# Second attention: the rotary part of the scores as two fp32r products of stacked parts

## The reference, cut to what matters

```
kv = (ckv_all @ w_kvb).reshape(B, Lk, H_D, NOPE_D + V_D)
k_nope, vals = jnp.split(kv, [NOPE_D], axis=-1)
keys = jnp.concatenate([k_nope, jnp.broadcast_to(kpe_all[:, :, None, :], (B, Lk, H_D, ROPE_D))], axis=-1)
qf = jnp.concatenate([q_nope, q_pe], axis=-1)
o_d = block_attention(qf, keys, vals, (NOPE_D + ROPE_D) ** -0.5).reshape(B, L, HALF_W)
```

## Time and profile before

| | us |
|---|---|
| time, three runs | 1636.16, 1636.16, 1636.3 |
| median | 1636.16 |
| span of the profiled execution | 1631.4 |
| median less span | 4.8 |
| TensorE busy | 1590.6 |
| VectorE busy | 1078.2 |
| ScalarE busy | 733.7 |

### The profile page before, as it was taken

One profiled execution on the slowest core, in us unless ns is written; L12 is line 12 of the kernel. 1 busy time (PEld: TensorE's weight loads), 2 busy tenths in 40 slices (PEclk: granted clock), 3 DMA queues, 4 the chain that ended last, 5 costly groups with the idle time before them and its releaser, 6 DMA issues.

```text
span 1631.4 us, 27746 instructions
## 1 busy us (share of the span) xinstructions
PE 1590.6 (98%) x11361; PEld 1464.3 (90%) x11361; DVE 1078.2 (66%) x1872; ACT 733.7 (45%) x1303; POOL 37.1 (2%) x42
## 2 busy tenths in 40 slices
PE   6999999999999999999999999999999999999997
PEld 3588897799989999999999996778999999999997
DVE  5634662868857747856874557744888487587486
ACT  5435363646624414423545433344665154254254
POOL 0000000001000000000003002000100000000000
PEclk9999999999999999999999999999999999999999
DMA  9565423035455544545234202002532223133222
GB/s 320 191 220 187 156 80 101 16 94 119 124 159 156 152 119 128 151 125 155 72 111 149 78 30 77 27 1 60 122 83 85 72 78 99 57 96 86 78 65 91
DMA packets 239336, 178.21 MB, mean 109 GB/s; under 512 B 9429, under 2 KB 232843, under 8 KB 238572
## 3 DMA queue, kind: packets, MB, share of 16 engines
q1 hardware_dynamic: 236276, 171.19, 34.9%
q0 software_dynamic: 2016, 4.59, 2.0%
q10 hardware_dynamic: 920, 0.69, 0.2%
HBM read 163.37 MB, written 8.49 MB: 105 GB/s over the span
## 4 chain that ended last, share of the span: by engine, by line
PE 89%; DVE 3%; ACT 3%; SPq 2%; DMA 2%; issue 1%; ACTq 0%; DVEq 0%
PE ua L1119 7%; PE ub L1119 6%; PE ua L1121 6%; PE ua L1120 6%; PE ub L1121 6%; PE ub L1120 6%; PE ua L1583 6%; PE ua L1585 5%; PE ua L1584 5%; PE ub L1583 5%; PE ub L1585 5%; PE ub L1584 5%; PE pm L1033 2%; PE ua L1428 2%; PE ub L1428 2%; PE pt L1455 1%
## 5 line engine op out<-in xcount | busy, mean ns | idle before, releaser
L2178 ACT ACTIVATE whi<-weight_sums 128x1024 fp32r<-128x1024 f32 x88 | 93.2, 1059 | 72.1 <-DVE weight_sums L2867 47.2
L1583 PE MATMUL ua<-x_mixed_high,whi 128*128 128x322 f32 x352 | 110.6, 314 | 1.9 <-ACT snap L2252 1.9
L1583 PE MATMUL ub<-x_mixed_high,whi 128*128 128x322 f32 x352 | 111.0, 315 | 0.9 <-ACT snap L2252 0.9
L1585 PE MATMUL ua<-x_mixed_high,wlo 128*128 128x322 f32 x352 | 109.2, 310 | 0.0
L1585 PE MATMUL ub<-x_mixed_high,wlo 128*128 128x322 f32 x352 | 109.2, 310 | 0.0
L1584 PE MATMUL ub<-x_mixed_rest,whi 128*128 128x322 f32 x352 | 109.0, 310 | 0.0
L1584 PE MATMUL ua<-x_mixed_rest,whi 128*128 128x322 f32 x352 | 109.0, 310 | 0.0
L2840 DVE TENSOR_TENSOR wlo<-weight_sums,whi 128x1024 fp32r<-128x1024 f32 x88 | 107.2, 1218 | 1.5 <-ACT whi L2178 1.4
L1119 PE MATMUL ub<-hidden_high,whi 128*128 128x384 f32 (+1 forms) x324 | 101.7, 314 | 4.5 <-DVE x L2935 3.5
L1119 PE MATMUL ua<-hidden_high,whi 128*128 128x384 f32 (+1 forms) x324 | 101.1, 312 | 1.9 <-DVE x L2935 1.9
L1121 PE MATMUL ua<-hidden_high,wlo 128*128 128x384 f32 (+1 forms) x324 | 100.1, 309 | 0.0
(11 more groups left out here) (671 smaller groups left out, 4949.0 us busy)
## 6 DMA issues: line engine op xcount, KB each, us to landing
raw<-in_w_ffn_in SPq DMA_DIRECT2D x88, 512.0 KB, 5.6
mod_late<-in_w_mod SPq DMA_DIRECT2D x24, 1024.0 KB, 5.4
raw<-in_w_ffn_out SPq DMA_DIRECT2D x48, 384.0 KB, 4.4
modw<-in_w_mod SPq DMA_DIRECT2D x17, 1024.0 KB, 5.8
raw<-in_w_in_even SPq DMA_DIRECT2D x10, 1024.0 KB, 7.8
raw<-in_w_in_odd SPq DMA_DIRECT2D x7, 1024.0 KB, 5.6
mod_first<-in_w_mod SPq DMA_DIRECT2D x5, 1024.0 KB, 12.3
ssq<-sq POOLq DMA_DIRECT2D x14, 320.0 KB, 4.7
```

The source lines that it names most:

```text
L1583: pe.matmul(dst, wh[:, c], xh, start=first, stop=False, skip_group_check=True)
L1585: ins = pe.matmul(dst, wl[:, c], xh, start=False, stop=last, skip_group_check=True)
L2178: act.activation(ring(whi, g, w), src, ACT.Copy).then_inc(g_hi, 1)
```

## The change

The zero-padded planes go. In their place stand the rotary keys as high part and rest, each with the key in both halves of the rows, and the queries, for each head, as high part in one half of the rows and rest in the other half. A product over all 128 rows of such queries with the keys' high part adds high by high and rest by high; one with the keys' rest adds high by rest and rest by rest. A run of scores in the second attention so has three products, one in fp32 and two in fp32r, where it had two in fp32.

ScalarE gets five more copies behind its 17 (one of the keys, four of queries). VectorE gets five subtractions: those of the keys and of head 0 ahead of the first Hyena tile, those of heads 1 to 3 ahead of the tiles 1 to 3. TensorE waits for all five ahead of the second attention. VectorE writes the rotary keys once in place of twice, and GpSimd's zero fill goes; its count moves to the fill just before it. The new query buffers take the places of `cq` and `sq`, the rest of the keys overwrites the keys.

```
-        kpz = ta("kpz", [P, 2, NKEY])
+        kr_hi = ta("rotary_keys_high", [P, NKEY], F32R)
+        kr_lo = ta("rotary_keys_rest", [P, NKEY], F32R)
+        kr = sb("rotary_keys", [P, NKEY], at=sb_at["rotary_keys_rest"])
...
+        qr = [sb("rotary_queries_even_heads", [P, 2, T], F32R, at=sb_at["cq"]),
+              sb("rotary_queries_odd_heads", [P, 2, T], F32R, at=sb_at["sq"])]
...
             for c in (0, LS + 1, UW - 2):
-                pool.memset(uh[:, :, c:c + 1], 0.0)
-            pool.memset(kpz[:, :, :], 0.0).then_inc(s_zero, 1)
+                ins = pool.memset(uh[:, :, c:c + 1], 0.0)
+            ins.then_inc(s_zero, 1)
...
-            pe.wait_ge(l_rq, 2)
+            pe.wait_ge(l_rq, 2 + 5)
             pe.wait_ge(y_f, 3)
-            attention(1, lambda h, t: [qn[:, h, t], qp[:, h // 2, t]], lambda h, t: [kn[:, h, t], kpz[:, h % 2, t]],
+            attention(1, lambda h, t: [qn[:, h, t], qr[h % 2][:, h // 2, t], qr[h % 2][:, h // 2, t]],
+                      lambda h, t: [kn[:, h, t], kr_hi[:, t], kr_lo[:, t]],
...
+            act.wait_ge(l_rk, 1)
+            act.activation(kr_hi[:, :], kr[:, :], ACT.Copy).then_inc(l_ev, 1)
+            for h in range(4):
+                rows = slice(64 * (h % 2), 64 * (h % 2) + 64)
+                act.wait_ge(l_rq, h // 2 + 1)
+                act.activation(qr[h % 2][rows, h // 2], qp[rows, h // 2], ACT.Copy).then_inc(l_ev, 1)
             for c in range(4):
                 act.wait_ge(y_f, c + 1)
...
-                    for a in range(2):
-                        rows = slice(64 * a, 64 * a + 64)
-                        ins = dve.tensor_copy(kpz[rows, a, 0:PAST], pm[rows, PAST:2 * PAST])
-                    ins.then_inc(l_c, 1)
+                    dve.tensor_copy(kr[:, 0:PAST], pm[:, PAST:2 * PAST]).then_inc(l_c, 1)
...
-            for a in range(2):
-                rows = slice(64 * a, 64 * a + 64)
-                dve.tensor_tensor(kpz[rows, a, PAST:PAST + LS], rot2[rows, 0, :], rot2[rows, 1, :], ALU.add)
-                ins = dve.tensor_copy(kpz[rows, a, PAST + LS:NKEY], kp[rows, LS:T])
-            ins.then_inc(l_rk, 1)
+            dve.tensor_tensor(kr[:, PAST:PAST + LS], rot2[:, 0, :], rot2[:, 1, :], ALU.add)
+            dve.tensor_copy(kr[:, PAST + LS:NKEY], kp[:, LS:T]).then_inc(l_rk, 1)
...
+            def rotary_query_rest(h):
+                rows, across = (slice(0, 64), slice(64, P))[::(1, -1)[h % 2]]
+                dve.wait_ge(l_ev, 17 + h + 2)
+                dve.tensor_tensor(qr[h % 2][across, h // 2], qp[rows, h // 2], qr[h % 2][rows, h // 2].bitcast(F32),
+                                  ALU.subtract).then_inc(l_rq, 1)
+
+            def rotary_rest(c):
+                if c == 0:
+                    dve.wait_ge(l_ev, 17 + 1)
+                    dve.tensor_tensor(kr_lo[:, :], kr[:, :], kr_hi[:, :].bitcast(F32), ALU.subtract).then_inc(l_rq, 1)
+                    rotary_query_rest(0)
+                elif c < 4:
+                    rotary_query_rest(c)
...
             for c in range(4):
+                rotary_rest(c)
                 dve.wait_ge(y_mm, c + 1)
```

More of the change, by code:

```diff
@@ L533, in build_program @@
         l_mm = sem("mla_projected")
-        l_ev = sem("mla_copied")
-        l_rq = sem("mla_queries_rotated")
+        l_ev = sem("mla_copied_and_rounded")
+        l_rq = sem("mla_queries_rotated_and_rests")
         q_ld = m_early[0:4]
```

## The result

The changed kernel takes 1626.6 us (median of four runs, 1625.22 to 1628.91) against 1636.16 us before: the ratio is 0.9947, with a 95% interval of 0.9935 to 0.9959. A second measurement of both gives 1626.31 against 1634.14 us, a ratio of 0.9949 (0.9934 to 0.9963). So the change gains 0.5%, 9.6 us in the first measurement and 7.8 in the second; 1627.6 us was forecast, in a range of 1626.0 to 1630.0.

The account below looks back on a forecast made before the run. TensorE, busy 98% of the span, was taken as the bound; 14 long jobs at 0.59 us (8.2) plus 0.4 for the prompt job save 8.6 us, so 1636.16 becomes 1627.6 us, range 1626.0 to 1630.0.

Parts of the forecast that it names:

- The price of a product: Second attention's scores: 512 fp32r columns take 0.232 us, 256 take 0.12, so a long job saves 0.59 us.
- The smaller estimate: Second attention's scores: 512 fp32r columns take 215.7 ns by the skill's formula, so a long job saves 0.64 us.
- Which jobs count: Second attention: 14 of 16 long jobs save 0.59 us each, 8.2 us; the first two only wait longer.
- the prompt job: Second attention's job of four heads, 128 columns each: scores go from 0.90 to 0.51 us, saving 0.4 us.
- The other bound: Prompt job in the second attention: no saving, if 128 columns cost 0.12 us as 256 do.
- 4.8 us were said to lie around the span: Whole kernel before: median 1636.16 us against a span of 1631.4 us; the difference was to stay.
- The cover: Ahead of the second attention: idle times hide the added copies and subtractions, with some 0.28 us over; counted at nothing.
- The switch between formats: Rival, inside score accumulations: 64 switches at 0.19 us each cost 12.2 us, time 1639.8 us; chance 0.06.
- The clock: Rival: 1.9 us idle before the first transposition lowers the clock, losing 1.7 us, time 1629.3 us; chance 0.10.
- VectorE was not late: Rival: rests overrun idle times of 1.1 us, first softmax up to 0.8 us late, time 1628.4 us; chance 0.10.
- The change does what it says: Rival denied here: each fp32r score product runs like one fp32 instruction, nothing gained, time 1636.2 us; chance 0.07.

## Why the prediction was right

**The price of a product.** 512 columns in fp32r were put at 0.232 us, on the line through two rows of another part of the kernel; the block became 2.00 us, as 1.29 + 0.70 has it. Without its fp32r products a block took 1.29 us, so the pair costs 0.355 and, with 256 columns at 0.12, 512 columns 0.235. The smaller estimate from the Trainium skill, "TensorE: Matmul & The Clock Gate", section "Wait — 56ns, not 53.3ns?" (0.64 a job, a block of 1.94), is not reached here.

**Which jobs count.** Fourteen long jobs, not sixteen: the stretch fell by 8.15 us, and 14 x (2.58 - 2.00) + 0.05 = 8.17. That two jobs' savings vanish ahead of the first softmax, while the same work costs its full price later, is shown by the pair of experiments that left rotary products out.

**The term that was mis-sized** is the prompt job: 0.4 us forecast, 0.05 measured. Its products of 128 columns cost 0.106 us and not 0.064; the line through 256 and 384 columns was carried below its ends, where the price is close to flat. The other bound, none if 128 columns cost what 256 do, was the better value. With it the sum would have been 8.2 in place of 8.6. The forecast span, 1622.8, met 1622.6 in part by luck, because the 0.67 us ahead of the stretch made up for these 0.4 us.

**A reading that was off** without touching the sum: 4.8 us were said to lie around the span. In the four runs of the changed kernel that list span and time together it is 1.9 to 2.9 us (1625.22 - 1622.6 = 2.6 in the profiled one). So the profiled execution before was probably some 2 us faster than the median it was set beside. The forecast subtracts its 8.6 us from the median and does not depend on this.

**The cover.** ScalarE's copies, VectorE's five subtractions and TensorE's wait for them were counted at nothing. Making them alone cost nothing that shows (74.29 us against 74.30), and the idle time left ahead of the tiles 2 and 3, 0.26 and 0.25, is what the rows gave (0.28). One more subtraction at each place cost 1.26 us.

**The rivals.** The switch between formats has no price within 0.01 us a job. The clock did not fall behind 1.8 us of idle time; it fell behind 3.2 in the one execution that had it, at a cost of 1.6 us, so this rival was near. The prediction judged it by the length of the gap alone (2.4 us did harm, 1.9 did none), and the waits near 50 us, where 2.10 us did harm and 2.51 did none, show that this is not enough; 1.8 us did none in six profiles of six. VectorE was not late. The change does what it says.

## What to carry to other kernels

Count a saving only in the repetitions in which its engine sets the pace: of 16 like jobs, two gained nothing here, since another engine's chain ended last there. Price a product from rows of the same format on both sides of its size. Outside them a line is a guess: here it held above its rows (512 columns) and failed below them (128), where the nearest row was the better value. Work that is to hide in idle times should be laid beside each of these times one by one; after such a change, the remaining idle time says what the next addition costs, and a grown one ahead of it may be worth a reordering.

## What the runs showed of the hardware that was not expected

Below 256 columns an fp32r product hardly gets cheaper in this kernel: 0.106 us at 128 columns, 0.11 at 192, 0.12 at 256, against about 0.235 at 512. At 128 columns it costs what one of the two instructions of an fp32 product does (0.112), so two fp32r products gain next to nothing over one fp32 product there (1.74 us for the prompt's block in place of 1.79). Mixing both formats in one accumulation was free within 0.01 us a job. In one execution 1.4 us less work ahead of a wait made the kernel's stretch 1.63 us longer, through the clock. And the same wait near 50 us was followed by a lower clock in three profiles and not in two, without regard to which wait was the longer.
